# Norm factors multiplied in on ScalarE inside the seven-product loop, a reordered loop entry, and a last projection whose second half comes out token by row

## The chip, the cores and the metric

One core of a Trainium2 chip runs the whole program in one launch. The metric is device time in microseconds (us). Instructions run on TensorE (PE; PEld is its weight load), VectorE (DVE), ScalarE (ACT), GpSimd (POOL) and SyncE (SP, which here only issues transfers). ScalarE and GpSimd issue transfers too.

## The reference, cut to what matters

A token sequence of 1024 with width 1024 passes through two blocks. The first ends in a feed-forward part; the second has a retention layer and a differential attention layer:

```python
up = causal_depthwise_conv(rms_norm(x, norm2_g) @ w_up, ffn_dw_w)      # 2 x 2816 channels
gate, val = jnp.split(up, 2, axis=-1)
x = x + (jax.nn.silu(gate) * val) @ w_down
# layer 0 of the second block: retention
x = x + rmsnorm((retention(...) * silu(gate)) @ w_out_a, post_norm[0])
# layer 1: differential attention
q, gate = split(rmsnorm(x, pre_norm[1]) @ w_in_b)
k, v = split(rmsnorm(x, kv_norm) @ w_kv)
y = (rmsnorm(diff_attention(q, k, v, lam), sub_norm_b) * (1 - lambda_init) * silu(gate)) @ w_out_b
x = x + rmsnorm(y, post_norm[1])                                       # the output
```

All of it is float32. `pre_norm[1]` and `kv_norm` are factors per input row of `w_in_b` and `w_kv`; `post_norm[1]` is a factor per output channel.

## The kernel before, in words

Activations lie with channels on the 128 partitions and tokens along the free axis: `A` has 8 tiles of 128 x 1024. Every float32 product is made of three fast ones (`mm3`): operands are split in a high part (`HH`, `WH`) and the rest (`HL`, `WL`). Weights come in units of 128 x 2048 floats, 1 MB each. In most phases a unit is transferred twice, by the SyncE queue to `RAW` and by GpSimd's queue to `WH`, and DVE then makes `WL` = `RAW` - `WH` (`low_part`, L269). `RAW` has one buffer, `WH` and `WL` have two. A new `RAW` transfer waits until the previous `low_part` is done; a new `WH` transfer waits until TensorE has begun the unit in the other buffer.

The feed-forward part has three stages. Its first four weight tiles are plain products (`ffn_first`). The other 18 tiles, t = 4 to 21, go through the seven-product loop (`up_pe`, `up_act`, `up_dve`): seven products M0 to M6 of 12 matmuls each replace eight, on sums of quarters of the weights ("pieces", built by GpSimd into `WLF`, split by ScalarE into `WH` and by DVE into `WL`, L1993) and on sums of quarters of the activations ("mixes", `XF`, built by GpSimd at L2115, split into `XH` and `XL`, L1981). M4 waits for ScalarE's copy `m2` of bank 0, M5 for DVE's `q`, M6 for DVE's `r` (L2201). The convolution taps of a tile are DVE's L2002; the next tile but one may not begin before they are done. The first tile of the loop is `j` = 0, so the second (`j` = 1) waits for the taps of plain tile 3. The third stage (`ffn_last`, `down_pe`) is the down projection in 22 units of 48 matmuls; ScalarE makes `WH` there (L2281) and DVE `WL` (L2286). The stage also reloads `A` and brings in the 22 tiles that the loop stored (`us_in`).

During this third stage the 16 units of `w_in_b` and `w_kv` get their norm factors: GpSimd's queue loads a unit to `gs` (two buffers), DVE multiplies it in two instructions (`gain_unit`, L2482), and GpSimd's queue stores it to the DRAM tensor `gu` (`gains_pool`), from where the attention phase reads its weights.

The differential attention runs over eight heads; in its last head (`diff_last`) parts of the last projection are slipped in. The last projection (`w_out_b`, `last_pe`) works on 8 output tiles of 128 channels, and does tokens 0 to 511 first, then tokens 512 to 1023. The sum of squares over channels is a product with a matrix of ones; then come a logarithm and an exponential on ScalarE, and for each of 8 tiles DVE's L632 (times factor and root) and L637 (plus `x`), and the stores.

## Time and profile before

| | us |
|---|---|
| median of 3 runs | 2733.58 (2727.04 to 2734.06) |
| the profiled execution | 2728.09 |
| its span, first to last instruction | 2726.4 |
| TensorE busy | 2652.7 |
| DVE busy | 1677.9 |
| ScalarE busy | 875.2 |
| GpSimd busy | 494.9 |

TensorE is busy nearly all the time, so the stages are read for the places where it is not, or where it is at the lower of its two clock levels. Busy time of the other engines matters only at such places.

### The profile page before, as it was taken

How to read it: one execution, taken by the hardware profiler on the slowest of the kernel's cores; microseconds unless marked ns; L12 is line 12 of the kernel's file. 1: busy time of each engine (PE TensorE's matmuls, PEld its weight loads, DVE VectorE, ACT ScalarE, POOL GpSimd, SP SyncE). 2: the span in 40 equal slices, each digit the busy share in tenths (PEclk: the TensorE clock that was granted, in tenths of full speed). 3: DMA queues.
4: the chain of work that ended last, by engine and by line, in shares of the span. 5: the costliest groups of instructions: out<-in, count | busy, mean ns of one | idle time of the engine just before them, and what ended most of it. 6: DMA issues, size and time to landing. Idle time of an engine off the chain costs nothing.

```text
span 2726.4 us, 35637 instructions
## 1 busy us (share of the span) xinstructions
PE 2652.7 (97%) x13108; PEld 2138.8 (78%) x13124; DVE 1677.9 (62%) x2240; ACT 875.2 (32%) x1580; POOL 494.9 (18%) x423
## 2 busy tenths in 40 slices
PE   9999989989999999999999999999999999999987
PEld 7767757877888878788888888888877888888775
DVE  8955563768888865445444345345376666666655
ACT  5333341333444433232112112112144444444441
POOL 0899900153333200121000000000000000000000
PEclk9999999999999999999999999999999999999999
DMA  5211114322222389742222222222244222222124
GB/s 194 77 63 61 52 57 150 113 101 78 85 77 85 150 333 340 264 172 91 77 92 77 77 92 77 77 92 77 78 154 143 78 77 77 77 77 77 58 78 155
DMA packets 59944, 300.42 MB, mean 110 GB/s; under 512 B 7648, under 2 KB 8800, under 8 KB 32224
## 3 DMA queue, kind: packets, MB, share of 16 engines
q1 hardware_dynamic: 34160, 154.53, 16.0%
q0 software_dynamic: 14976, 109.06, 11.8%
q10 hardware_dynamic: 10736, 35.86, 3.4%
q8 instruction: 48, 0.79, 0.1%
q14 instruction: 24, 0.20, 0.0%
HBM read 245.93 MB, written 45.09 MB: 107 GB/s over the span
## 4 chain that ended last, share of the span: by engine, by line
PE 78%; DMA 7%; DVE 6%; issue 2%; ACT 1%; POOL 1%; SPq 0%; DVEq 0%; ACTq 0%; POOLq 0%
PE OBB L253 9%; PE OBB L255 9%; PE OBB L254 9%; DMA gu<-gs 6%; PE PB L253 4%; PE PB L255 4%; PE PB L254 4%; PE TBB L253 4%; PE TBB L255 4%; PE TBB L254 4%; PE TBB L979 3%; PE PB L1028 2%; PE OBB L1093 2%; PE PB L1945 2%; PE PB L1947 2%; PE PB L1946 2%
## 5 line engine op out<-in xcount | busy, mean ns | idle before, releaser
L253 PE MATMUL OBB<-HH,WH 128*128 128x512 f32 x752 | 306.3, 407 | 4.2 <-issue 3.0
L255 PE MATMUL OBB<-HH,WL 128*128 128x512 f32 x752 | 295.6, 393 | 0.0
L254 PE MATMUL OBB<-HL,WH 128*128 128x512 f32 x752 | 295.3, 393 | 0.0
L3143 POOL DMA_DIRECT2D WH<-units x56 | 30.4, 542 | 1184.4 <-PE OBB L253 734.2
L253 PE MATMUL PB<-HH,WH 128*128 128x512 f32 x560 | 227.0, 405 | 1.6 <-DVE hc L903 1.0
L255 PE MATMUL PB<-HH,WL 128*128 128x512 f32 x560 | 218.3, 390 | 0.0
L254 PE MATMUL PB<-HL,WH 128*128 128x512 f32 x560 | 218.1, 389 | 0.0
L269 DVE TENSOR_TENSOR WL<-RAW,WH 128x2048 fp32r<-128x2048 f32 x72 | 170.0, 2361 | 73.1 <-DMA WH<-units 71.3
L1228 ACT ACTIVATE E<-PB,small 128x128 f32<-128x128 f32 (+3 forms) x192 | 141.1, 738 | 224.5 <-DVE small L1324 218.2
L1324 DVE TENSOR_REDUCE small<-PB 128x1 f32<-128x128 f32 (+3 forms) x192 | 138.7, 752 | 61.2 <-PE PB L1046 61.1
L253 PEld LDWEIGHTS OBB<-HH,WH 128*128 128x128 f32 x752 | 142.9, 190 | 32.4 <-issue 4.0
L255 PEld LDWEIGHTS OBB<-HH,WL 128*128 128x128 f32 x752 | 142.4, 189 | 32.0
L2107 POOL TENSOR_TENSOR WLF<-RAW 128x512 f32<-128x512 f32 x90 | 124.6, 1387 | 232.9 <-PE PB L1947 109.8
L254 PEld LDWEIGHTS OBB<-HL,WH 128*128 128x128 f32 x752 | 143.0, 190 | 26.6
L2789 ACT ACTIVATE vr<-OBB,rtok 128x256 f32<-128x256 f32 x32 | 15.3, 477 | 353.1 <-PE OBB L255 353.1
L253 PEld LDWEIGHTS PB<-HH,WH 128*128 128x128 f32 x560 | 105.2, 188 | 28.9 <-issue 5.0
L3176 POOL TENSOR_TENSOR cacc<-cacc,prod 128x498 f32<-128x498 f32 (+29 forms) x94 | 126.4, 1345 | 0.0
L254 PEld LDWEIGHTS PB<-HL,WH 128*128 128x128 f32 x560 | 105.2, 188 | 25.7 <-issue 4.8
L3165 POOL TENSOR_TENSOR prod<-hc,par 128x498 f32<-128x498 f32 (+29 forms) x94 | 123.3, 1312 | 6.8
L255 PEld LDWEIGHTS PB<-HH,WL 128*128 128x128 f32 x560 | 105.1, 188 | 22.3
L1945 PE MATMUL PB<-XH,WH 128*128 128x512 f32 x252 | 101.0, 401 | 11.7 <-ACT m L2155 8.1
L1993 DVE TENSOR_TENSOR WL<-WLF,WH 128x512 fp32r<-128x512 f32 x90 | 105.1, 1170 | 0.0
(456 smaller groups left out, 6277.8 us busy)
## 6 DMA issues: line engine op xcount, KB each, us to landing
RAW<-units SPq DMA_DIRECT2D x78, 1024.0 KB, 4.9
WH<-units POOLq DMA_DIRECT2D x56, 1024.0 KB, 5.1
RAW<-ups SPq DMA_DIRECT2D x18, 1024.0 KB, 4.8
gs<-units POOLq DMA_DIRECT2D x16, 1024.0 KB, 7.7
gu<-gs POOLq DMA_DIRECT2D x16, 1024.0 KB, 10.8
RAW<-gu SPq DMA_DIRECT2D x16, 1024.0 KB, 4.9
WH<-gu POOLq DMA_DIRECT2D x16, 1024.0 KB, 5.1
ub<-V SPq DMA_DIRECT2D x22, 512.0 KB, 2.6
```

Of the source, the lines that this page charges most:

```text
L253: first = pe.e.matmul(out, wh, xh, start=start, stop=False)
L254: pe.e.matmul(out, wh, xl, start=False, stop=False)
L255: return pe.e.matmul(out, wl, xh, start=False, stop=stop), first
L269: dve.e.tensor_tensor(WL[s][:, :], RAW[:, :], WH[s][:, :].bitcast(F32), ALU.subtract).then_inc(unit_split, 1)
L979: mm = pe.e.transpose(dst[:, c * P:(c + 1) * P], src(b), c_("ident"))
L1228: e.activation((E0, E1)[c][:, 0:n], PB[c][:, 0:n], ACT.Exp, bias=small[:, c, t:t + 1], accum_out=small[:, 2 + c, t:t + 1]).then_inc(act_do ...
L1324: e.tensor_reduce(small[:, c, t:t + 1], PB[c][:, 0:(t + 1) * P], AX, ALU.max, negate=True).then_inc(dve_done, dve.mark(f"m{c}_{t}"))
L1945: pe.e.matmul(bank(j, n), wh, XH[p][:, k, :], start=p < 4 and k == 0, stop=False, skip_group_check=True)
L1993: dve.e.tensor_tensor(piece(WL, p), source, piece(WH, p).bitcast(F32), ALU.subtract).then_inc(dve_done, dve.mark(f"w{p}_{j}"))
L2107: pool.tensor_tensor(piece(WLF, p), raw_quarter(t % 2, a), raw_quarter(t % 2, b), op).then_inc(summed, 1)
L3165: ins = pool.tensor_tensor(prod[:, n % 2, 0:b - a], hc[:, c, a - d:b - d], weight.to_broadcast([P, b - a]), ALU.mult)
L3176: pool.tensor_tensor(cacc[:, c, a:b], cacc[:, c, a:b], prod[:, n % 2, 0:b - a], ALU.add).then_inc(conv_taps, 1)
```

## The change

Three parts.

First, the norm factors. `gains_pool` and DVE's `gain_unit` go. For the tiles t = 5 to 20 of the seven-product loop ScalarE's `gain_unit` multiplies one unit in place, as 16 instructions of 128 x 128 with a factor per partition, between piece 2 and piece 3 of the tile. SyncE's queue stores the unit to `gu`, waits until that has landed, and loads the next one to `gs`, which now has one buffer.

Second, the entry of that loop. Mixes 3 and 5 are built by DVE (`mix_sum`) and no longer by GpSimd; the copy `m2` and the combinations `q`, `r`, `ra` of the first loop tile come ahead of the taps of plain tile 3; the Silu and the gate product of plain tile 3 come behind.

Third, the last projection. Tokens 0 to 511 are still made with channels on the partitions, from units `U_WOB` to `U_WOB + 3`, cut so that the first two hold output tiles 0 to 3. Tokens 512 to 1023 are made with tokens on the partitions: the activation tile is the stationary operand and a weight row block of 512 columns the moving one, in four units `U_WOB + 4` to `+ 7`, each used for all four token tiles `j`. So the last matmuls of the four token tiles fall close together. Squares are then summed along the free axis by ScalarE, the root is a number per partition, and DVE needs two L632-like and two L637-like instructions for each token tile. The input `x` for these tokens is loaded at the start of the last head and turned there by TensorE (`x_turn_pe`, 32 transposes), in place of six filler matmuls; ScalarE takes it out of the banks. Eight units are brought in, where five were. The output is assembled from two tensors by the host.

```diff
+            for n in range(4):
+                slot = unit(pe, U_WOB + 4 + n)
+                for j in range(4):
+                    if n == 0 and j == 2:
...
+                        pe.e.wait_ge(dve_done, at_mark(pe, "dve", "acc7"))
+                        pe.e.matmul(OB[0], ones[:, :], last_square(0), start=True, stop=True).then_inc(
+                            pe_done, pe.mark("total"))
+                    if n == 0 and j < 3:
+                        pe.e.wait_ge(dve_done, at_mark(pe, "dve", f"y{2 * j + 1}_0"))
+                    if n == 0 and j == 3:
+                        pe.e.wait_ge(act_done, at_mark(pe, "act", "ln"))
+                    tokens = slice(HALF + j * P, HALF + (j + 1) * P)
+                    for b in range(2):
+                        for r in range(2):
+                            k, c = 2 * n + r, r * 1024 + b * HALF
...
+                for n in range(4):
+                    e.dma_start(xf[:, 2 * n:2 * n + 2, :], xs_pieces()[n][:, :, half_of(0)]).then_inc(x_again[n], 16)
...
+                e.wait_ge(pe_done, at_mark(act, "pe", f"z{j}_{b}"))
+                if j:
+                    e.wait_ge(act_done, at_mark(act, "act", f"zq{j - 1}_{b}"))
+                e.activation(sql[:, b, :], TOKEN_BANKS[j][b], ACT.Square, scale=D ** -0.5,
+                             accum_out=small[:, b, j:j + 1]).then_inc(act_done, act.mark(f"zq{j}_{b}"))
...
+                e.wait_ge(dve_done, at_mark(act, "dve", f"bias{j}"))
+                e.activation(small[:, 3, j:j + 1], small[:, 1, j:j + 1], ACT.Ln, bias=small[:, 2, j:j + 1]).then_inc(
+                    act_done, act.mark(f"zl{j}"))
+                e.wait_ge(act_done, at_mark(act, "act", f"zl{j}"))
+                e.activation(small[:, 4, j:j + 1], small[:, 3, j:j + 1], ACT.Exp, scale=-0.5).then_inc(
+                    act_done, act.mark(f"zr{j}"))
...
+            def token(j, b):
+                e.wait_ge(act_done, at_mark(dve, "act", f"zr{j}"))
+                out = A[:, 2 * j + b, half_of(1)]
+                e.scalar_tensor_tensor(out, TOKEN_BANKS[j][b], small[:, 4, j:j + 1], gainb[:, half_of(b)],
+                                       ALU.mult, ALU.mult).then_inc(dve_done, dve.mark(f"zs{j}_{b}"))
+
+            def token_add(j, b):
+                e.wait_ge(dve_done, at_mark(dve, "dve", f"zs{j}_{b}"))
+                out = A[:, 2 * j + b, half_of(1)].rearrange("p (k n) -> p k n", n=P)
+                e.tensor_tensor(out, out, xt[b][:, :, j * P:(j + 1) * P], ALU.add).then_inc(
+                    dve_done, dve.mark(f"z{j}_{b}"))
+
+            low_part(dve, U_WOB + 2)
...
+            low_part(dve, U_WOB + 5)
+            for k in range(4):
+                tile(k)
+            low_part(dve, U_WOB + 6)
+            for k in range(4, KT):
...
+            low_part(dve, U_WOB + 7)
+            e.wait_ge(tok_in[2], 16)
+            bias(0)
+            for j in range(4):
+                token(j, 0)
+                token(j, 1)
+                if j < 3:
+                    bias(j + 1)
+                token_add(j, 0)
+                token_add(j, 1)

...
-                for n in range(3):
-                    act.e.dma_start(XRB[:, 2 * n:2 * n + 2, :], xs_pieces()[n]).then_inc(x_again[n], 16)
-                act.e.dma_start(XRB[:, 6, :], xs_pieces()[3][:, 0, :]).then_inc(x_again[3], 16)
-                act.e.dma_start(xr7[:, :], xs_pieces()[3][:, 1, :]).then_inc(x_again[3], 16)
             for k in range(KT):
...
             if not more and not forget:
+                unit(pe, U_WOB + 1)
                 for k in (4, 5):
-                    whole_pe(pe, U_WOB, k, k == 4)
+                    pe.e.wait_ge(dve_done, at_mark(pe, "dve", f"lo{k}"))
+                    last_whole(pe, k)
...
+                low_part(dve, U_WOB + 1)
...
+            for m in range(4):
+                c = m * HALF + (k - 4) * P
+                last, first = mm3(pe, FIRST_BANKS[m], WH[slot][:, c:c + P], WL[slot][:, c:c + P],
+                                  HH[:, k, half_of(0)], HL[:, k, half_of(0)], k == 4, k == KT - 1)
...
+        TURN_BANKS = {1: ((0, TB[1]), (1, HIGH_PB[0])), 2: ((2, TB[1]), (3, HIGH_PB[0]), (4, HIGH_PB[1])),
+                      3: ((5, TB[1]), (6, DB[:, :]), (7, HIGH_PB[0]))}
...
+        def x_load(act):
+
+            act.e.wait_ge(spilled, 16 + 64)
+            for n in range(2):
+                act.e.dma_start(xt[n][:, :, :], io["xs"].rearrange("(k p) s -> p k s", p=P)[
+                    :, 4 * n:4 * n + 4, half_of(1)]).then_inc(tok_in[n], 16)
+            act.e.dma_start(gainb[:, :], io["gain"]).then_inc(tok_in[2], 16)
...
+            for k, bank in TURN_BANKS[t]:
+                act.e.wait_ge(pe_done, at_mark(act, "pe", f"xt{k}"))
+                act.e.activation(xt[k // 4][:, k % 4, :], bank, ACT.Copy).then_inc(act_done, act.mark(f"xe{k}"))

...
-            for p in (3, 4, 5):
-                mix_high(act, p)
...
             e.wait_ge(pe_done, at_mark(act, "pe", "v3"))
             for p in (4, 5):
                 piece_high(act, p, 1, UP_FIRST)
+            mix_high(act, 5)
             gate_value(3)
+            e.wait_ge(dve_done, at_mark(act, "dve", "x1"))
+            e.wait_ge(summed, FIRST_SUMS["x6"])
+            e.wait_ge(pe_done, done_in("pe", UP_PHASES[0], "M0_0"))
+            e.activation(m2[:, 0, :], bank(0, 0), ACT.Copy).then_inc(act_done, act.mark("m2_f"))
             mix_high(act, 6)
             e.wait_ge(summed, FIRST_SUMS["p6"])
             piece_high(act, 6, 1, UP_FIRST)
...
             product(2)
+            mix_sum(dve, 3, "h1")
             for p in range(4):
                 piece_low(dve, p, 1, UP_FIRST, None)
+            mix_sum(dve, 5, "h5")
             mix_low(dve, 3)
+            scaled(3)
...
-            mix_low(dve, 5)
-            scaled(3)
             for p in (4, 5):
                 piece_low(dve, p, 1, UP_FIRST, None)
+            mix_low(dve, 5)
...
+                e.tensor_tensor(out, bank(0, product), b, op).then_inc(dve_done, dve.mark(name))
+
+            e.wait_ge(act_done, at_mark(dve, "act", "m2_f"))
+            combined("q_f", 1, None, qb[:, 0, :], m2[:, 0, :], ALU.add)
+            mix_low(dve, 6)
+            combined("r_f", 2, "q_f", rb[:, 0, :], qb[:, 0, :], ALU.subtract)
+            piece_low(dve, 6, 1, UP_FIRST, None)
+            combined("ra_f", 3, "r_f", rb[:, 0, :], rb[:, 0, :], ALU.add)
             taps_of(3)
...
-            for p, name in ((3, "h1"), (4, "h3"), (5, "h5"), (6, "v3")):
+            for p, name in ((4, "h3"), (6, "v3")):
...
+            def gain_unit(j, i):
+
+                e.wait_ge(gain_in, counted(act, i, 32, 16 * j))
+                for n in range(2 * KT):
+                    part = gs[:, n * P:(n + 1) * P]
+                    ins = e.activation(part, part, ACT.Copy, scale=p_(("pre_b", "kvn")[n // KT], n % KT, 1))
+                ins.then_inc(act_done, act.mark(f"gain_{j}"))
...
+                            e.wait_ge(dve_done, done_in("dve", "ffn_first", f"cg_{tag(UP_FIRST - 1)}"))
+                            e.activation(G0[:, :], G0[:, :], ACT.Silu).then_inc(act_done, act.mark("si_f"))
+                        else:
+                            gain_unit(j, i)
...
+                j, r = t % 2, t - UP_FIRST - 1
+                if 0 <= r < 2 * DIFF_HEADS:
+                    sp.wait_ge(act_done, up_at("act", t, f"gain_{j}"))
+                    sp.dma_start(io["gu"][r], gs[:, :]).then_inc(gain_out, 16)
                 if t < FF_TILES - 1:
-                    sp.wait_ge(summed, 10 + 5 * (t + 1 - UP_FIRST))
+                    sp.wait_ge(summed, FIRST_SUMS["p6"] + 5 * (t + 1 - UP_FIRST))
...
+                if r + 1 < 2 * DIFF_HEADS:
+                    if t == UP_FIRST:
+                        sp.wait_ge(u_out[(t - 1) % 2], 16 * (t // 2))
+                    else:
+                        sp.wait_ge(gain_out, 16 * (r + 1))
+                    sp.dma_start(gs[:, :], io["units"][U_DIFF + r + 1]).then_inc(gain_in, 16)
...
-                pool.dma_start(gs[r % 2][:, :], io["units"][U_DIFF + r]).then_inc(gain_in[r % 2], 16)
-
-            pool.wait_ge(pe_done, up_at("pe", FF_TILES - 1, "M0_1"))
-            load(0)
-            load(1)
-            for r in range(2 * DIFF_HEADS):
-                pool.wait_ge(dve_done, done_in("dve", "ffn_last", f"gain{r}1"))
-                pool.dma_start(io["gu"][r], gs[r % 2][:, :]).then_inc(gain_out[r % 2], 16)
-                if r + 2 < 2 * DIFF_HEADS:
-                    pool.wait_ge(gain_out[r % 2], 16 * (r // 2 + 1))
-                    load(r + 2)
-
-        def gain_unit(dve, r):
-            dve.e.wait_ge(gain_in[r % 2], 16 * (r // 2 + 1))
-            for j in range(2):
-                part = gs[r % 2][:, j * 1024:(j + 1) * 1024].rearrange("p (k n) -> p k n", k=KT)
-                dve.e.tensor_tensor(part, part, p_(("pre_b", "kvn")[j]).unsqueeze(2).to_broadcast([P, KT, P]),
-                                    ALU.mult).then_inc(dve_done, dve.mark(f"gain{r}{j}"))
```

On DVE, at the entry of the loop, this stood before, from the piece differences of the first loop tile on (XL: rest of a mix; WL: rest of a piece; rbx and par: scaling and taps of plain tile 3):

```order
L1993 TENSOR_TENSOR WL_58<-WLF_128,WH_56 128x512 x4
L1981 TENSOR_TENSOR XL_143<-XF_147,XH_139 128x2048
L1981 TENSOR_TENSOR XL_144<-XF_148,XH_140 128x2048
L1981 TENSOR_TENSOR XL_145<-XF_149,XH_141 128x2048
L2063 TENSOR_TENSOR TBB<-TBB,rbx 128x1024
L2063 TENSOR_TENSOR OBB<-OBB,rbx 128x1024
L1993 TENSOR_TENSOR WL_59<-RAW,WH_57 128x512 x2
L2002 SCALAR_TENSOR_TENSOR G_151<-TBB,par,G_151 128x1023
L2002 SCALAR_TENSOR_TENSOR G_151<-TBB,par,G_151 128x1022
L2002 SCALAR_TENSOR_TENSOR V_152<-OBB,par,V_152 128x1023
L2002 SCALAR_TENSOR_TENSOR V_152<-OBB,par,V_152 128x1022
L1981 TENSOR_TENSOR XL_146<-XF_150,XH_142 128x2048
```

And this stands there now (L2055: `mix_sum`; L2190: `combined` of the first loop tile):

```order
L2055 TENSOR_TENSOR XF_151<-A 128x2048
L2072 TENSOR_TENSOR WL_57<-WLF_131,WH_55 128x512 x4
L2055 TENSOR_TENSOR XF_153<-A 128x2048
L2060 TENSOR_TENSOR XL_147<-XF_151,XH_143 128x2048
L2146 TENSOR_TENSOR TBB<-TBB,rbx 128x1024
L2146 TENSOR_TENSOR OBB<-OBB,rbx 128x1024
L2060 TENSOR_TENSOR XL_148<-XF_152,XH_144 128x2048
L2072 TENSOR_TENSOR WL_58<-RAW,WH_56 128x512 x2
L2060 TENSOR_TENSOR XL_149<-XF_153,XH_145 128x2048
L2190 TENSOR_TENSOR qb<-PB,m_159 128x512
L2060 TENSOR_TENSOR XL_150<-XF_154,XH_146 128x2048
L2190 TENSOR_TENSOR rb<-PB,qb 128x512
```

Two mixes have come in, and `qb` and `rb`, for which M5 and M6 wait, stand ahead of the taps, which begin three instructions after the last row shown.

On ScalarE, this stood before in the second tile of the loop (m: the copy for which M4 waits; WH: pieces 0 to 3 of the next tile, then 4 and 5):

```order
L2155 ACTIVATE m_155<-OBB 128x512
L1987 ACTIVATE WH_56<-WLF_128 128x512 x4
L1987 ACTIVATE WH_57<-RAW 128x512 x2
L2166 ACTIVATE carry<-epsc 128x1
L2167 ACTIVATE V<-OBB,par 128x1024
L2171 ACTIVATE carry<-epsc 128x1
L2172 ACTIVATE G<-TBB,par 128x1024
```

And now:

```order
L2258 ACTIVATE m_159<-OBB 128x512
L2066 ACTIVATE WH_55<-WLF_131 128x512 x3
L2240 ACTIVATE gs<-gs,par 128x128 x16
L2066 ACTIVATE WH_55<-WLF_131 128x512
L2066 ACTIVATE WH_56<-RAW 128x512 x2
L2276 ACTIVATE carry<-epsc 128x1
L2277 ACTIVATE V<-OBB,par 128x1024
L2281 ACTIVATE carry<-epsc 128x1
```

The 16 instructions on `gs` stand between piece 2 and piece 3, and what follows them on ScalarE waits for them.

At the end of the program DVE had this before, for the last five of eight output tiles of the second half of the tokens (L632 times factor and root, L637 plus `x`), all of it behind the last matmul and the root:

```order
L632 SCALAR_TENSOR_TENSOR tmn<-OBB,par,rbn 128x512
L637 TENSOR_TENSOR A<-tmn,XRB 128x512
L632 SCALAR_TENSOR_TENSOR tmn<-PB,par,rbn 128x512
L637 TENSOR_TENSOR A<-tmn,XRB 128x512
L632 SCALAR_TENSOR_TENSOR tmn<-PB,par,rbn 128x512
L637 TENSOR_TENSOR A<-tmn,XRB 128x512
L632 SCALAR_TENSOR_TENSOR tmn<-TBB,par,rbn 128x512
L637 TENSOR_TENSOR A<-tmn,XRB 128x512
L632 SCALAR_TENSOR_TENSOR tmn<-TBB,par,rbn 128x512
L637 TENSOR_TENSOR A<-tmn,xr_55 128x512
```

And now, for the last two token tiles (L648: `token`, L654: `token_add`, L642: `bias`):

```order
L648 SCALAR_TENSOR_TENSOR A<-TBB,small,gainb 128x512 x2
L642 TENSOR_TENSOR small<-small,epsc 128x1
L654 TENSOR_TENSOR A<-A,xt_78 128x512
L654 TENSOR_TENSOR A<-A,xt_79 128x512
L648 SCALAR_TENSOR_TENSOR A<-OBB,small,gainb 128x512 x2
L654 TENSOR_TENSOR A<-A,xt_78 128x512
L654 TENSOR_TENSOR A<-A,xt_79 128x512
```

Eight tiles' worth of instructions behind the last matmul have become one token tile's: the last three rows, four instructions.

## Rows read from the trace of the kernel before

**Rows 1.** The page's head and its first part.

```profile
span 2726.4 us, 35637 instructions
...
PE 2652.7 (97%) x13108; PEld 2138.8 (78%) x13124; DVE 1677.9 (62%) x2240; ACT 875.2 (32%) x1580; POOL 494.9 (18%) x423
```

**Rows 2.** Busy time by stretch: length, engines, granted clock, DMA share, GB/s.

```profile
602.40:627.40 25.00, 13.28 (x38) 10.18 (x38) 22.05 (x23) 10.81 (x14) 10.98 (x7) 0.73 0.27 106
627.40:952.80 325.40, 325.40 (x1426) 267.48 (x1425) 277.14 (x304) 137.19 (x218) 111.44 (x83) 1.00 0.26 96
952.80:1165.00 212.20, 203.66 (x881) 165.58 (x880) 120.18 (x112) 65.33 (x70) 24.92 (x33) 0.99 0.83 306
2563.80:2639.00 75.20, 66.94 (x370) 51.32 (x371) 43.96 (x72) 34.78 (x77) 0.53 (x1) 0.95 0.04 15
2639.00:2706.50 67.50, 66.31 (x291) 54.23 (x290) 31.96 (x40) 10.39 (x17) 1.58 (x3) 1.00 0.52 187
2706.50:2726.40 19.90, 1.86 (x5) 0.38 (x3) 10.92 (x16) 1.91 (x3) 0.00 (x0) 0.68 0.29 106
```

**Rows 3.** Timeline at the loop's entry: start, us, instruction, idle before and releaser.

```profile
578.83 6.86 DVE L1993 TENSOR_TENSOR WL<-WLF,WH 128x512 fp32r<-128x512 f32 x4
...
599.19 2.68 DVE L1981 TENSOR_TENSOR XL<-XF,XH 128x2048 fp32r<-128x2048 f32 x1 [4.39 <-ACT XH L1975]
...
606.38 2.59 DVE L2002 SCALAR_TENSOR_TENSOR G<-TBB,par,G 128x1023 f32<-128x1023 f32 x2
...
610.60 0.80 PE L1945 MATMUL PB<-XH,WH 128*128 128x512 f32 x1 [8.07 <-ACT m L2155]
...
619.00 0.80 PE L1945 MATMUL PB<-XH,WH 128*128 128x512 f32 x1 [3.66 <-DVE qb L2201]
```

**Rows 4.** Timeline of the second loop tile, ScalarE's piece 3 and DVE.

```profile
640.01 0.63 ACT L1987 ACTIVATE WH<-WLF 128x512 fp32r<-128x512 f32 x1 [2.27 <-POOL WLF L2107]
...
641.66 0.68 DVE L2201 TENSOR_TENSOR qb<-OBB,qb 128x512 f32<-128x512 f32 x1
...
646.57 0.70 DVE L2201 TENSOR_TENSOR TBB<-TBB,qb 128x512 f32<-128x512 f32 x1 [1.36 <-PE TBB L1947]
```

**Rows 5.** Timeline of ScalarE: a 128 x 128 instruction and its successor.

```profile
2627.40 0.31 ACT L3012 ACTIVATE sqd<-ot 128x128 f32<-128x128 f32 x1
2627.61 0.19 ACT L3012 ACTIVATION_READ_ACCUMULATOR sqd<-ot 128x1 f32 x1
```

**Rows 6.** Waits in the down projection (952 to 1165 us).

```profile
DVE gs L2482 <- DMA gs<-units: 72.7, 14, 8.6
...
PE PB L253 <- DVE WL L2286: 4.9, 4, 1.7
```

**Rows 7.** Transfers of 900 to 1165 us: KB each, median us to landing.

```profile
gs<-units POOLq DMA_DIRECT2D x16, 1024.0 KB, 7.7
gu<-gs POOLq DMA_DIRECT2D x16, 1024.0 KB, 10.8
```

**Rows 8.** Transfers of 640 to 900 us, the same columns.

```profile
RAW<-ups SPq DMA_DIRECT2D x14, 1024.0 KB, 4.8
ub<-V SPq DMA_DIRECT2D x13, 512.0 KB, 2.6
```

**Rows 9.** Timeline of the last projection and of the end.

```profile
2639.72 0.53 POOL L3143 DMA_DIRECT2D WH<-units  x1 [42.85 <-PE TBB L253]
...
2648.59 2.29 DVE L269 TENSOR_TENSOR WL<-RAW,WH 128x2048 fp32r<-128x2048 f32 x1 [3.56 <-DMA WH<-units]
...
2650.93 0.50 PE L253 MATMUL OBB<-HH,WH 128*128 128x512 f32 x1 [1.19 <-DVE WL L269]
...
2652.06 0.53 POOL L3143 DMA_DIRECT2D WH<-units  x1 [11.81 <-PE OBB L253]
...
2659.05 2.29 DVE L269 TENSOR_TENSOR WL<-RAW,WH 128x2048 fp32r<-128x2048 f32 x1 [1.63 <-DMA WH<-units]
...
2720.56 0.69 DVE L637 TENSOR_TENSOR A<-tmn,xr 128x512 f32<-128x512 f32 x1
```

381 lines of the change are left out of this document (194 added, 187 removed).

## The prediction

> **What bounds the kernel now.** I read the head of the page first: TensorE is busy 2652.7 of 2726.4 us [rows 1]. So a gain can only come from places where it waits, where its clock is low, or from the end, where it has finished. The busy time by stretch shows the three that the change touches [rows 2]. At the loop's entry, 602.4 to 627.4 us, it is busy 13.3 of 25.0 us at a mean granted clock of 0.73. In the down projection, 952.8 to 1165, it is busy 203.7 of 212.2 us while the DMA engines are 0.83 busy. After 2706.5 it has next to nothing to do for 19.9 us. In between, the loop has no gap at all: 325.4 of 325.4 us at clock 1.00, with DMA at 0.26. The reader is to see that the same transfers and multiplications that crowd one stage would have room in the other.
>
> **The norm factors leave the down projection.** Removed are 32 DVE instructions, 16 loads and 16 stores of 1 MB. DVE waited 72.7 us for loads to `gs`, up to 8.6 at a time, and what is queued behind such a wait is `WL` of the next unit, for which TensorE then waited 4.9 us [rows 6]. The other waits there come from `RAW` and `us_in` landing late on full queues: a 1 MB load took 7.7 us and a store 10.8 [rows 7], against 4.8 for a load in the loop [rows 8]. All in all TensorE loses 212.2 - 203.7 = 8.5 us by gaps and 0.01 x 212 = 2 us by the clock [rows 2], together 10.6. The upper end of the gain is 10.6. The lower end is 4: a first gap (the fill of the stage) and the one while `A` and the stored tiles come back may stay, since those transfers stay. I take 9, since without 32 MB the stage needs about half of what it moves now.
>
> **They enter the loop.** Per tile ScalarE gets 16 instructions of 128 x 128. Such an instruction lasts 0.31 us and the next starts 0.21 us after it [rows 5]; 16 x 0.21 + 0.1 = 3.5 us. Behind them are queued pieces 3, 4 and 5, for which DVE waits, and behind those on DVE the combinations that free the banks. In the row, piece 3 starts at 640.01, 2.27 us after ScalarE was last busy (637.74) [rows 4]. With the factors between, it starts at 637.74 + 3.5 = 641.2, so 1.2 us late. DVE's instruction after piece 3, at 641.66, becomes about 1.2 us late, and DVE then waits 1.36 us for TensorE at 646.57 [rows 4]. The delay ends there, and TensorE sees nothing: cost 0 per tile, hidden by DVE's wait. Without that cover it would be 1.2 x 16 = 19 us. ScalarE itself has room: 137 of 325 us busy, plus 16 x 3.5 = 56 [rows 2]. The first loop tile that does this may start it late; I put 0.5 us.
>
> The Trainium skill, "ScalarE: Activation LUTs", section Rules for kernel authors, says that multiplications belong on VectorE and that an instruction on ScalarE is to be budgeted at some 0.3 us plus 0.83 ns per element. An estimate by it is 16 x 0.41 = 6.5 us per tile; piece 3 would then be 4.2 us late, DVE about 2 us late behind the cover, and the loop would stand near the edge. The start-to-start time of the row decides against that figure, and I keep 3.5.
>
> Transfers in the loop grow by 2 MB per tile of 325.4/17 = 19.1 us. The store comes first, then the load waits until the store has landed, then ScalarE multiplies: a ring. With 4.8 us for a load, about the same for a store (0.5 MB took 2.6) [rows 8], and 3.5 for ScalarE it is 13 us, under 19.1. The load also stands behind `RAW` of a later tile on SyncE's queue and behind GpSimd's last piece, so it may land near the moment when ScalarE wants it; up to 1 us late would still be covered.
>
> **The entry.** TensorE waits 8.07 us for `m` and 3.66 us for `qb` [rows 3]. M4 to M6 take 3 x 12 x 0.228 = 8.2 us at the loop's pace (325.4 us for 17 x 84 matmuls [rows 2]), but took 25 from 602.4; 16.8 us are lost, 11.7 in gaps and 5 by the clock. Now `m` stands ahead of the Silu and waits only for M0 and GpSimd's mix 6. GpSimd has two mixes fewer, so `m` is ready before 602.4 and the first gap goes. Then DVE is late next. From 578.8 it has, in its new order: a mix (2.5), four pieces (6.9 [rows 3]), a mix (2.5), four rests of mixes (2.7 each [rows 3], the first one longer), scaling 2.4 (2048 columns, at 0.68 us for 512 [rows 4] less three starts), two pieces 2.4, `q`, `r`, `ra` (0.7 each [rows 4]) and piece 6 (1.7, as one of the four at 578.8), and the taps, 2 x 2.6 [rows 3]; together 37 us, to 616. A mix of 128 x 2048 is not in the trace on DVE; the nearest row is the rest of a mix, same size, same number of operands, 2.7 us. `q` comes at about 605 and costs nothing, `r` and piece 6 at about 610, some 2 us late. M0 of the next tile waits for the taps and its piece 0: 616.5, against 627.2 before. The gap before it is about 4 us, like the one at 619.00; the two gaps of before cost 5 us by the clock, so this one 2.2 to 2.5; I put 2.2. The gain is 627.2 - 616.5 - 2.2 = 8.5; I take 9 since the low clock may be shorter. Bounds: 12 if DVE is never slowed by GpSimd's additions and the clock stays up, 5 if each DVE step there is a fifth slower.
>
> **The last projection.** The matmuls are as many as before, and six units of 48 still come behind the last head. What changes is the end. Before, from 2706.5, a product with ones, a logarithm, an exponential and 16 DVE instructions up to 2721.25 [rows 9], then 5.15 us until the last store has landed and the program ends at 2726.4 [rows 1]. Now the last token tile needs, after the last matmul, a square of 512 columns (0.6, as the 0.63 in [rows 4], and 0.2 to read its sum [rows 5]), a logarithm and an exponential of one column (0.2 each at least, as that read; with waits 0.7), and DVE's four instructions. DVE takes 2.9 us per token tile (four of 0.7 [rows 9], and a small one), and TensorE delivers one each 12 x 0.228 = 2.7 us, so DVE lags a little: it ends about 4.9 us after the last matmul. With 5.15 us for the store this makes 10.0 instead of 19.9: gain 9.9 (8 to 11).
>
> What it costs: units follow each other every 48 x 0.228 = 10.9 us, and 2 MB must come in for each. A `WH` transfer issued beside its `RAW` landed 8.9 us after issue in one place (2639.72 to 2648.59), and TensorE stood 1.19 us; it landed after 7.0 us in the other (2652.06 to 2659.05), and TensorE did not stand [rows 9]. With 1.1 us before the issue and 2.3 for `WL`, the unit is there 12.3 or 10.4 us after the one before began. Before, only two hand-overs had this form; now there are five or six, one of them beside 2 MB of `x`. Bounds: -1 (no gap at all) and +9 (six gaps of 1.4 instead of one, and 2 for `x`). I take +1.5, nearer the faster row, as nothing else was on the queues there either. Two exchanges in the last head, `low_part` of the second unit ahead of the last transposes and 32 transposes for six fillers, lie where TensorE stands 8.3 of 75.2 us anyway [rows 2]; at most as long as 32 wide matmuls, 7 us, at least minus 2. I put +0.5.
>
> The Trainium skill, "DMA: Bandwidth & Descriptors", section Anatomy of one DMA, gives 2.0 us plus bytes over 436 GB/s. An estimate by it for the pair is 2.0 + 4.8 = 6.8 us, so a unit every 10.2 us and no gap; the last stage would cost 0 and the sum be 1.5 lower. The row of 7.0 agrees with it, the row of 8.9 does not.
>
> **The sum**, against the profiled execution's own 2728.1: - 9 (down projection) + 0.5 (loop) - 9 (entry) - 9.9 (end) + 1.5 + 0.5 (last projection, last head) = 2701.7. The median of the runs stands 5.5 us above that execution, and the runs spread from 2727.0 to 2734.1, so I forecast 2703.
>
> **The rivals.** (a) The ring becomes the bound. If loads and stores in the loop take what they took in the down projection, the ring is 7.7 + 10.8 + 3.5 + 0.7 for two issues = 22.7 us, 3.6 above a tile. Over 15 rounds that is +54: 2757, slower. It decides from a ring of 19.1 us on, so from 15 us for store and load. Against it stands the DMA share of 0.26 in the loop. (b) The last projection becomes bound by its transfers at the slower row: +9 instead of +1.5, 2710 to 2712. For it speaks that each late unit makes both transfers of the next start together again. (c) The entry hardly gains, because GpSimd and DVE disturb each other and the low clock returns: 2707 to 2709. (d) The gaps of the down projection stay, being made by `A` and `us_in`: 2708. (e) ScalarE's factors are not covered, 1.2 us per tile: 2722, still faster. (f) The change does nothing: only if (e) and (b) come together.
>
> **How the numbers follow.** Forecast, all three gains within their bounds: 0.62, 2695 to 2709. One of (b), (c), (d) or two of them in part: 0.24, up to 2717. (e): 0.06. (a): 0.05. No change: 0.03. The range 2694 to 2716 holds somewhat over 8 in 10. A measurement of this kernel tells 0.3%, 8 us, from no change: faster 0.92, same 0.03, slower 0.05.
>
> **What would show it.** In the profile after: the PE wait for `m` gone, and one gap of 3 to 5 us before the second loop tile; loop tiles 19.1 us apart, and no SyncE or ScalarE wait for `gs` that reaches TensorE; fewer than 3 us of gaps in the down projection; the last matmul about 10 us before the end; gaps before units of the last projection of 0 to 1.5 us. Tiles 20 us or more apart would show (a) or (e), and regular gaps of over 1 us behind 2640 would show (b).

## The result, and the profile after

| | before | after |
|---|---|---|
| median of the runs, us | 2733.82 (4 runs) | 2693.96 (4 runs, 2691.51 to 2696.82) |
| ratio, 95% interval | | 0.9864 (0.9852 to 0.9876) |
| the same once more, later | 2731.70 (9 runs) | 2699.76 (5 runs), 0.9874 (0.9856 to 0.9891) |
| the profiled execution, us | 2728.09 | 2696.82 |
| its span | 2726.4 | 2695.2 |

One of the four runs of the kernel before took 11960.6 us; it is left out of the ratio. The change makes the kernel 1.26 to 1.36 per cent faster, by 34 to 37 us. The forecast was 2703 with a range from 2694 to 2716: right in sign, with a time 3 to 9 us too long. The first median, 2693.96, lies on the lower edge of the range, the second inside it. The two medians of this one kernel are 5.8 us apart, so a difference of less than some 6 us between two medians below says little.

The head of the page, beside [rows 1]:

```profile
span 2695.2 us, 35949 instructions
...
PE 2647.1 (98%) x13124; PEld 2139.3 (79%) x13140; DVE 1642.8 (61%) x2211; ACT 951.5 (35%) x1858; POOL 466.3 (17%) x386
```

Busy time by stretch of the changed kernel, for the same six places as [rows 2] (length, engines, granted clock, DMA share, GB/s):

```profile
602.40:614.80 12.40, 8.67 (x38) 6.55 (x37) 12.33 (x12) 4.71 (x8) 9.75 (x5) 0.97 0.22 81
614.80:943.40 328.60, 328.58 (x1426) 269.82 (x1427) 280.48 (x312) 209.53 (x476) 109.09 (x80) 0.99 0.50 193
943.40:1146.00 202.60, 200.58 (x881) 164.83 (x880) 84.28 (x80) 65.59 (x70) 7.21 (x3) 1.00 0.46 167
2546.15:2621.10 74.95, 66.17 (x387) 53.28 (x388) 45.34 (x72) 38.55 (x85) 1.06 (x2) 0.93 0.22 78
2621.10:2688.50 67.40, 67.15 (x293) 54.47 (x291) 38.99 (x50) 12.48 (x30) 2.65 (x5) 1.00 0.65 227
2688.50:2695.20 6.70, 0.00 (x0) 0.00 (x0) 3.90 (x8) 1.19 (x5) 0.00 (x0) 0.82 0.62 233
```

The reader is to see three stretches that shrank: the entry from 25.0 to 12.4 us, the down projection from 212.2 to 202.6, the end from 19.9 to 6.7. The loop's DMA share rose from 0.26 to 0.50 and the down projection's fell from 0.83 to 0.46: the 32 MB have moved to where there was room. The loop is 3.2 us longer, and the factors are not the reason: from the first matmul of its fourth tile to its last matmul it takes 287.57 us in both profiles (tiles 19.19 us apart). The 3.2 us are the second tile, 22.14 us instead of 19.19 behind the gap at 614.82 (granted clock 0.50 from 614.8 to 620.5), and 0.2 by where the stretches were cut.

One profile against one profile hides what chance does. So I cut every profiled run at the same five matmuls, by their rows: the first of the seven-product loop, the first of the down projection (`UH`; the wait before it falls in the loop's column), the product with ones of the retention phase (`sqr`, after its first norm), the first scores of the last head, and the last matmul of the projection. The differences of their times, in us:

| run | to the loop | loop | down projection and on | attention | last head and projection | end | span |
|---|---|---|---|---|---|---|---|
| before | 591.35 | 363.90 | 1064.18 | 544.37 | 142.75 | 19.85 | 2726.4 |
| after | 591.46 | 354.41 | 1054.59 | 545.69 | 142.32 | 6.73 | 2695.2 |
| after_again | 596.24 | 352.90 | 1054.59 | 542.42 | 142.44 | 6.71 | 2695.3 |
| undo_gains | 596.69 | 355.17 | 1069.24 | 545.43 | 143.63 | 6.84 | 2717.0 |
| undo_entry | 597.84 | 362.18 | 1054.53 | 543.95 | 140.43 | 6.67 | 2705.6 |
| undo_last | 591.24 | 353.42 | 1054.56 | 544.39 | 142.30 | 17.29 | 2703.2 |
| work_only | 591.50 | 354.05 | 1054.37 | 544.28 | 141.98 | 6.72 | 2692.9 |
| moves_only | 592.38 | 357.45 | 1066.69 | 545.37 | 140.60 | 6.71 | 2709.2 |
| order_only | 594.38 | 358.31 | 1054.41 | 544.27 | 141.81 | 6.72 | 2699.9 |
| entry2 | 591.61 | 356.64 | 1054.40 | 543.75 | 143.45 | 6.65 | 2696.5 |
| mixes_dve | 597.52 | 352.16 | 1054.66 | 545.66 | 142.76 | 6.64 | 2699.4 |
| mixes_dve2 | 595.51 | 354.72 | 1054.54 | 544.06 | 140.53 | 6.64 | 2696.0 |
| gains_x15 | 592.38 | 367.89 | 1055.58 | 545.15 | 142.93 | 6.67 | 2710.6 |
| gains_x2 | 596.10 | 387.00 | 1056.41 | 543.98 | 139.03 | 6.98 | 2729.5 |

Read by column, it says what is chance. No run changed the part to the loop, and it lies between 591.2 and 597.8. The third column is 1054.4 to 1054.7 in all eight runs that have nothing extra in the loop or in that stage; there a difference of 1 us is real. The loop's column has 1 to 2 us of chance (352.9 and 354.4 for the same kernel), and that of the last head and projection more: 139.0 to 143.6 in the runs that have the new last projection.

The entry, in the timeline of the changed kernel (beside [rows 3]):

```profile
599.68 0.60 ACT L2126 ACTIVATE m<-PB 128x512 f32<-128x512 f32 x1 [3.06 <-issue]
...
600.07 3.39 DVE L2060 TENSOR_TENSOR XL<-XF,XH 128x2048 fp32r<-128x2048 f32 x1
603.38 0.68 DVE L2190 TENSOR_TENSOR qb<-PB,m 128x512 f32<-128x512 f32 x1
...
606.68 0.68 DVE L2190 TENSOR_TENSOR rb<-PB,qb 128x512 f32<-128x512 f32 x1
...
608.56 0.47 PE L2012 MATMUL PB<-XH,WH 128*128 128x512 f32 x1 [0.48 <-DVE WL L2072]
...
614.82 0.77 PE L2012 MATMUL OBB<-XH,WH 128*128 128x512 f32 x1 [3.28 <-DVE WL L2072]
```

`m` is ready 10 us earlier than before, TensorE waits 0.48 us for piece 6 and 3.28 us before the second loop tile, and for nothing else there.

A loop tile of the changed kernel, ScalarE and DVE (beside [rows 4, 5]):

```profile
704.98 4.78 ACT L2240 ACTIVATE gs<-gs,par 128x128 f32<-128x128 f32 x16
709.67 0.61 ACT L2066 ACTIVATE WH<-WLF 128x512 fp32r<-128x512 f32 x1
...
710.32 0.69 DVE L2072 TENSOR_TENSOR WL<-WLF,WH 128x512 fp32r<-128x512 f32 x1 [1.85 <-ACT WH L2066]
...
714.00 0.70 DVE L2314 TENSOR_TENSOR TBB<-TBB,qb 128x512 f32<-128x512 f32 x1 [0.58 <-PE TBB L2014]
```

The 16 factors take 709.67 - 704.98 = 4.69 us, and piece 3 starts 2.3 us later in the tile than before (15.16 us behind its first matmul, 12.84 before). DVE's wait for TensorE, 1.36 us before [rows 4], is down to 0.58, but it is still there. Before, DVE waited twice for TensorE behind piece 3; the first wait, which is now gone, is this one:

```profile
643.85 0.70 DVE L2201 TENSOR_TENSOR OBB<-TBB,rb 128x512 f32<-128x512 f32 x1 [0.92 <-PE TBB L1947]
```

The transfers of the loop after (614 to 942 us, beside [rows 7, 8]):

```profile
gs<-units SPq DMA_DIRECT2D x16, 1024.0 KB, 7.0
gu<-gs SPq DMA_DIRECT2D x16, 1024.0 KB, 3.9
RAW<-ups SPq DMA_DIRECT2D x15, 1024.0 KB, 4.9
```

And all that TensorE still waits for in the down projection (942.7 to 1146 us, beside [rows 6]):

```profile
PE PB L253 <- DVE WL L2405: 1.8, 1, 1.8
...
PE PB L253 <- DVE UL L2390: 0.3, 1, 0.3
```

### The profile page after: what moved, and what is told of

It reads as the page before. It is cut to its first block, busy times and chain, and to the rows that moved or that the text cites. A ratio compares the mean times of both kernels' runs of the same rounds, so it can differ in the third digit from the quotient of the medians.

```text
span 2695.2 us, 35949 instructions
## 1 busy us (share of the span) xinstructions
PE 2647.1 (98%) x13124; PEld 2139.3 (79%) x13140; DVE 1642.8 (61%) x2211; ACT 951.5 (35%) x1858; POOL 466.3 (17%) x386
## 4 chain that ended last, share of the span: by engine, by line
PE 86%; DVE 6%; issue 2%; ACT 1%; DMA 1%; SPq 0%; DVEq 0%; ACTq 0%; POOLq 0%
PE OBB L253 10%; PE OBB L255 9%; PE OBB L254 9%; PE PB L253 5%; PE PB L255 5%; PE PB L254 5%; PE TBB L253 4%; PE TBB L255 4%; PE TBB L254 4%; PE TBB L994 3%; PE PB L1043 2%; PE OBB L1110 2%; PE PB L2012 2%; PE PB L2014 2%; PE PB L2013 2%
## 5 line engine op out<-in xcount | busy, mean ns | idle before, releaser
L253 PE MATMUL OBB<-HH,WH 128*128 128x512 f32 x736 | 300.2, 408 | 3.2 <-issue 3.0
L255 PE MATMUL OBB<-HH,WL 128*128 128x512 f32 x736 | 289.4, 393 | 0.0
L254 PE MATMUL OBB<-HL,WH 128*128 128x512 f32 x736 | 289.2, 393 | 0.0
L269 DVE TENSOR_TENSOR WL<-RAW,WH 128x2048 fp32r<-128x2048 f32 x75 | 178.1, 2375 | 83.8 <-DMA WH<-units 82.2
L253 PE MATMUL PB<-HH,WH 128*128 128x512 f32 x528 | 214.2, 406 | 2.8 <-DVE HL L415 1.8
L255 PE MATMUL PB<-HH,WL 128*128 128x512 f32 x528 | 205.8, 390 | 0.0
L254 PE MATMUL PB<-HL,WH 128*128 128x512 f32 x528 | 205.6, 389 | 0.0
L2405 DVE TENSOR_TENSOR WL<-RAW,WH 128x2048 fp32r<-128x2048 f32 x22 | 51.9, 2358 | 130.2 <-ACT WH L2400 130.1
L253 PEld LDWEIGHTS PB<-HH,WH 128*128 128x128 f32 x528 | 99.1, 188 | 28.4 <-issue 4.7
L254 PEld LDWEIGHTS PB<-HL,WH 128*128 128x128 f32 x528 | 99.2, 188 | 24.5 <-issue 4.5
L255 PEld LDWEIGHTS PB<-HH,WL 128*128 128x128 f32 x528 | 99.1, 188 | 21.2
```

The costliest lines, as they stand in the source:

```text
L253: first = pe.e.matmul(out, wh, xh, start=start, stop=False)
L254: pe.e.matmul(out, wh, xl, start=False, stop=False)
L255: return pe.e.matmul(out, wl, xh, start=False, stop=stop), first
L269: dve.e.tensor_tensor(WL[s][:, :], RAW[:, :], WH[s][:, :].bitcast(F32), ALU.subtract).then_inc(unit_split, 1)
```

## The experiments

All are edits of the changed kernel unless said otherwise; ratios are to the kernel before, measured beside it.

**undo_gains.** Part one of the change put back, parts two and three kept.

```diff
-                        else:
-                            gain_unit(j, i)
...
+                if u < 2 * DIFF_HEADS:
+                    gain_unit(dve, u)
...
+            gains_pool(pool)
```

> The changed kernel with only the norm factors put back where they were (DVE multiplies them in the down projection, GpSimd's queue moves the 32 MB); entry and last projection stay changed. The changed kernel's down projection has one gap of 1.76 us and clock 1.00, and between its start and the next phase it gained 9.6 us on the kernel before. My theory, that transfers and multiplications on full queues made the gaps: four or five gaps come back, DVE waits some 70 us for gs, and the kernel is 9 to 10 us slower than the changed one (2703 to 2706, profile 2705). Rival, that the gaps came from A and us_in as before and vanished only because the phase is entered with other leads: less than 3 us. ScalarE's share of the loop falls by some 75 us without any effect on TensorE.

Measured: 0.9915 (0.9902 to 0.9929), that is 11 to 14 us slower than the changed kernel. In the table it is the third column, 1069.24 against 1054.59. TensorE has eight gaps from its first matmul on, of 0.4 to 3.3 us, and DVE waits 77.5 us for `gs`. That the factors made the gaps holds; the size is somewhat larger than I had said, and larger than before the change (1064.18). Its five runs spread over 14 us (2704.28 to 2718.72), those of the changed kernel over 5 and 8, and its profile is of the slowest of the five.

**work_only** and **moves_only.** Which half of it makes the gaps, DVE's work or the transfers? Each is added alone to the changed kernel's down projection: in work_only two products of 128 x 1024 in place (the first two lines), in moves_only the loads and stores (the others).

```diff
+                if u < 2 * DIFF_HEADS:
+                    gain_work(dve, u)
...
+                    pool.dma_start(io["gx"][r - 2], gz[r % 2][:, :]).then_inc(extra_out[r % 2], 16)
...
+                    pool.dma_start(gz[r % 2][:, :], io["units"][U_DIFF + r]).then_inc(extra_in[r % 2], 16)
```

> The changed kernel with 32 extra DVE multiplications (128 x 1024 in place, two per unit of the down projection, where the factors stood before) and no extra transfer. Nothing is left out. By my theory, that the transfers made the gaps of the down projection, DVE's 16 x 2.4 = 38 us of work lie in its waits for ScalarE's WH (113 us in the changed kernel): at most 1 us slower than the changed kernel (2694 to 2695 as its own median; below 0.04%). Rival, that DVE's place in the chain WH, WL makes the gaps: 2.4 us more between WH and a second unit's WL, gaps of 1 us and more per unit, 5 to 14 us slower.

> The changed kernel with 16 extra loads and 16 extra stores of 1 MB by GpSimd's queue in the down projection (each store behind its load, two buffers, to a DRAM tensor that nobody reads), with no DVE work and no wait of any engine but GpSimd for them, before unit 17. Nothing is left out. By my theory gaps come back as with the whole part put back: 9 to 14 us slower than the changed kernel (2703 to 2708), with RAW and us_in landing late. Rival, DVE's waits for gs (72.7 us before) and its multiplications made the gaps: under 3 us.

Measured: work_only 0.9872 (0.9857 to 0.9887), third column 1054.37: nothing. moves_only 0.9932 (0.9918 to 0.9945), 16 to 19 us slower, more than the 9 to 14 I had put; its third column is 1066.69, 12 us more, and its first gap of 5.59 us adds 3 to 4.5 to the loop's column. Its issues, one of its waits and two of TensorE's rows:

```profile
RAW<-units SPq DMA_DIRECT2D x18, 1024.0 KB, 9.9
...
us_in<-ub SPq DMA_DIRECT2D x44, 256.0 KB, 8.7
```

```profile
ACT WH L2403 <- DMA RAW<-units: 34.1, 4, 13.2
```

```profile
949.83 0.79 PE L255 MATMUL PB<-UH,WH 128*128 128x512 f32 x1 [5.59 <-DVE WL L2408]
...
1004.06 0.77 PE L255 MATMUL PB<-UH,WH 128*128 128x512 f32 x1 [6.06 <-DVE UL L2393]
```

A load of `RAW` lands after 9.9 us, where in the changed kernel it takes 4.9. Both gaps end on DVE, which stands behind ScalarE; before the gap at 1004.06 ScalarE waited 13.2 us for such a load, before that at 949.83 it waited 9.8 us for `us_in`. So crowded transfers alone can make a loss, and DVE's work alone makes none. This path was in the kernel before too: ScalarE waited 15.18 us for `RAW` there, and TensorE's gap behind it was 2.73 us (at 1002.58).

The early loss of moves_only can't be taken over in size, since its extra stores begin at 935.20, those of the kernel before at 971.01. And moves_only has three gaps, the last at 1004, and none of the later ones. In its second part the extra transfers still run, the DMA engines are 0.85 busy (0.80 in the kernel before, 1030 to 1165 us), and TensorE has no gap:

```profile
1020.00:1130.00 110.00, 110.00 (x485) 90.70 (x485) 41.77 (x41) 31.16 (x32) 8.98 (x17) 1.00 0.85 303
```

In the kernel before TensorE stood there at 1093.43, 1116.89 and 1139.27 for 1.56, 1.34 and 0.32 us, and each time DVE had just come out of a wait for `gs`:

```profile
1112.28 2.36 DVE L2482 TENSOR_TENSOR gs<-gs,par 128x1024 f32<-128x1024 f32 x2 [8.60 <-DMA gs<-units]
1114.55 2.28 DVE L2286 TENSOR_TENSOR WL<-RAW,WH 128x2048 fp32r<-128x2048 f32 x1
1116.89 0.50 PE L253 MATMUL PB<-UH,WH 128*128 128x512 f32 x1 [1.34 <-DVE WL L2286]
```

ScalarE had `WH` ready long before (it waited for TensorE), so what was late was DVE's factor product behind the load, and `WL` behind that. Undo_gains has five such gaps, 5.1 us together, behind waits for `gs` of 5.2 to 9.6 us. So DVE's waits for `gs` [rows 6], which I had read as the first link, were the last link of 3.2 of the 4.9 us that TensorE waited for `WL`; 1.73 of them are the first gap, which stayed. This path needs the late load and DVE's work behind it, and neither half has it alone; no run adds only DVE's wait.

**gains_x2** and **gains_x15.** How much cover have the factors? Behind the 16 factors come 16 copies in place, 8 in gains_x15.

```diff
+                e.wait_ge(act_done, at_mark(act, "act", f"factor_{j}", i))
+                for n in range(16):
+                    part = gs[:, n * P:(n + 1) * P]
+                    ins = e.activation(part, part, ACT.Copy)
```

> The changed kernel with 16 more ScalarE instructions of 128 x 128 per loop tile (copies in place, factor 1), behind the 16 of the factors: nothing is left out. They take 4.7 us more per tile. By my theory the factors are covered only by DVE's wait for TensorE behind piece 3, of which 0.58 us is left: (4.7 - 0.6) x 16 = 66 us slower, tiles 23.3 us apart. Rival, the ring of store, load and ScalarE is what binds: 9.5 + 3.9 + 7.0 + 0.2 = 20.6 us per tile, 1.4 over 19.2, 21 us slower. Second rival, TensorE's buffers hide more than DVE's wait shows: less than 40.

> The changed kernel with 8 extra copies of 128 x 128 in place behind the factors of each loop tile. 16 such copies made piece 3 3.34 us later and the tile 1.97 us longer, so 1.37 us of lateness were hidden. If that is a fixed slack, 8 copies (1.7 us) cost 0.3 us per tile, 5 us in all; tiles 19.5 us apart. If instead a share of each added us reaches TensorE (59 per cent in that run), they cost 1.0 us per tile, 16 us in all.

Measured: gains_x2 0.9999 (0.9989 to 1.0008), 34 to 37 us slower than the changed kernel where my theory said 66; gains_x15 0.9917 (0.9901 to 0.9932), 12 to 14 us slower. ScalarE's rows of one tile of gains_x2, and TensorE's wait in it:

```profile
823.97 4.79 ACT L2240 ACTIVATE gs<-gs,par 128x128 f32<-128x128 f32 x16
828.78 3.31 ACT L2245 ACTIVATE gs<-gs 128x128 f32<-128x128 f32 x16
832.00 0.62 ACT L2066 ACTIVATE WH<-WLF 128x512 fp32r<-128x512 f32 x1
```

```profile
822.63 0.49 PE L2012 MATMUL PB<-XH,WH 128*128 128x512 f32 x1 [1.68 <-ACT m L2263]
```

Piece 3 comes 832.00 - 823.97 - 4.69 = 3.34 us later, and the tile takes 21.16 us instead of 19.19, 1.97 more. With 8 copies it is 1.75 us later and the tile 19.95, 0.76 more. So 1.0 to 1.4 us more than the factors would have stayed hidden, and none of my lines is right (all but 0.6; a fixed 1.37, so 0.3 per tile; 59 per cent, so 1.0 per tile). TensorE's wait for `m` suggests why DVE's 0.58 was not the whole cover: lateness passes from piece 3 to DVE's combinations, to the taps, to the Silu, and to the `m` behind it on ScalarE, and it reaches TensorE at M4. In gains_x15 most of the short waits end on DVE's `qb` instead. Both runs also pay at the first matmul of the down projection, which waits 4.4 and 4.8 us instead of 1.8. The ring did not bind: no wait for `gs` in either run.

**undo_entry** and **order_only.** Part two put back whole; and the new order kept with mixes 3 and 5 by GpSimd.

```diff
-            for p, name in ((4, "h3"), (6, "v3")):
+            for p, name in ((3, "h1"), (4, "h3"), (5, "h5"), (6, "v3")):
...
-            mix_sum(dve, 3, "h1")
-            mix_sum(dve, 5, "h5")
```

> The changed kernel with only the entry of the seven-product loop put back (GpSimd builds mixes 3 and 5, m, q, r behind the taps of plain tile 3). By my theory the gaps of 8 and 3.7 us and the low clock come back, so it is 11 us slower than the changed kernel (12.4 in the arrival of the second loop tile's M0, less what the low clock behind the one gap of now costs, 2.6): 2704 to 2707. Rival, that the factors on ScalarE or the other moves made the entry quick: under 5 us.

> The changed kernel with mixes 3 and 5 built by GpSimd again, but the new order kept (m, q, r ahead of the taps of tile 3). Before, GpSimd ended mix 6 at 604.2 and M4's operands m was 610.0 behind the gate product's copies and a Silu. By my theory (GpSimd's two mixes fewer are what brings mix 6, and with it m, ahead of TensorE) a gap of 4 to 5 us before M4 stays, with the low clock: 5 to 7 us slower than the changed kernel. Rival, the order alone does it: under 2 us slower.

Measured: undo_entry 0.9895 (0.9880 to 0.9910), 6 to 9 us slower, less than my 11 (12.4 less 2.6 is 9.8, so 11 was also a slip); loop column 362.18 against 352.9 to 354.4, 8 to 9 us. The two gaps came back (8.09 us for `m`, 3.23 for `qb`). order_only 0.9884 (0.9869 to 0.9899), column 358.31: 4 to 5 us, about half of it, and a little less than I had put. In order_only TensorE waits 3.33 us for `m` at 608.90, then 2.16 us before M0 of the second tile and 2.45 before its M4. The mixes and the order each carry a part.

**entry2, mixes_dve, mixes_dve2.** The gap of 3.28 us and the low clock behind it seemed worth another 4 to 5 us. Entry2 makes the value taps, then piece 0, then the gate taps (the first three lines); mixes_dve builds mixes 4 and 6 on DVE too (the last two); mixes_dve2 does both.

```diff
-            taps_of(3)
+            tap_marks(dve, 3, 1, V0, None, tag(3))
...
+                        low(0)
...
+            mix_sum(dve, 4, "h3")
...
+            mix_sum(dve, 6, "v3")
```

> A version meant to be faster. In the changed kernel the second loop tile's M0 waits 3.27 us for DVE's piece 0, which stands behind all four taps of plain tile 3, and the 1.2 GHz that follows costs 2.6 us. M0 writes a value bank, M1 is the first to write a gate bank. So DVE now does the value taps, piece 0 of that tile, then the gate taps and the other pieces; TensorE waits for the gate taps only before M1. By my theory M0 comes at 612.2 instead of 614.8, the gap is 0.6 us and the clock stays at 2.4 GHz: 4 to 5 us faster than the changed kernel. Rival, M1 now waits as long for the gate taps (ready 2.5 us later): a gain under 1 us.

> A version meant to be faster: mixes 4 and 6 are built by DVE too, so GpSimd builds no mix between tile 3's first product and the loop. In the changed kernel DVE is busy without a break from 578.7 to 632 us, and beside GpSimd's mixes its instructions are long: four piece differences 6.89 us (0.68 each alone), a rest of a mix 3.39 (2.28 alone). By my theory, that the entry is as long as DVE's work in it, DVE gets 2 x 2.28 us more and loses 4.2 + 2.2 + 1.1 us of slowing: 3 us less. M0 of the second loop tile then comes 3 us earlier, at TensorE's own pace, with no gap of over 0.5 us and no low clock there: 3 to 5.5 us faster than the changed kernel. Rival, GpSimd's next pieces move into the same time and slow DVE as the mixes did: under 1 us gained, or up to 2 us lost.

> The version just named together with the order of taps of the run entry2 (value taps, piece 0, gate taps). If DVE's backlog is what bounds the entry, the order of the taps only moves the wait, and this equals the version just named within 1 us. If its M0 still waits for the taps there, this one is up to 2.6 us faster.

> The changed kernel once more, beside the three that follow. Median 2693 to 2696, ratio to the kernel before 0.986.

Measured: entry2 0.9876 (0.9860 to 0.9891), mixes_dve 0.9871 (0.9852 to 0.9890), mixes_dve2 0.9868 (0.9851 to 0.9884), after_again 0.9874 (0.9856 to 0.9891), its median 2699.76 where I had put 2693 to 2696. None is faster than the changed kernel, where I had put 4 to 5 us for entry2 and 3 to 5.5 for mixes_dve. TensorE in entry2:

```profile
612.47 0.47 PE L2012 MATMUL OBB<-XH,WH 128*128 128x512 f32 x1 [0.77 <-DVE WL L2076]
...
629.28 0.80 PE L2012 MATMUL OBB<-XH,WH 128*128 128x512 f32 x1 [5.18 <-ACT m L2262]
```

M0 came 2.35 us earlier, as computed, and M4 of the same tile then waited 5.18 us for an `m` that stands behind DVE's and ScalarE's backlog. The wait had moved and grown, and the low clock came behind it (granted clock 0.50 from 629.28 to 634). The loop's column is 356.64, 2 to 4 us worse. In mixes_dve2 the same happened: M4 waited 5.23 us. In mixes_dve GpSimd's next piece (597.77 to 600.14) runs beside DVE's mix 6:

```profile
598.89 3.40 DVE L2055 TENSOR_TENSOR XF<-A 128x2048 f32<-128x2048 f32 x1
...
619.41 0.47 PE L2012 MATMUL OBB<-XH,WH 128*128 128x512 f32 x1 [2.54 <-DVE WL L2072]
...
633.09 0.50 PE L2012 MATMUL OBB<-XH,WH 128*128 128x512 f32 x1 [2.42 <-ACT m L2260]
```

M0 of the second tile came 1.5 us earlier behind the loop's first matmul (21.89 us, 23.37 in the changed kernel), not 3. Its loop column, 352.16, is at most 2 us better than the changed kernel's 352.9 to 354.4, which no ratio here can tell.

**undo_last.** Part three put back whole.

> The changed kernel with only the last projection (and its parts in the last head) put back. Last matmul to end: 6.7 us in the changed kernel, 19.9 before; I had forecast 10.0, from 4.9 us of DVE and 5.15 us for the last store as before. If the store's tail belongs to the old form of output, it is 5 us again here and the kernel is 13 to 14 us slower than the changed one (2706 to 2709). If the tail is chance from run to run, it is 2.7 here, and the kernel is 11 us slower. The one gap of 1.2 us before a unit comes back, too.

Measured: 0.9906 (0.9891 to 0.9921), 9 to 11.5 us slower; end column 17.29. DVE's last instruction ends at 2700.61, and the program ends 2.6 us later. With the same code the profile before needed 5.15: its slowest store landed after 4.3 us, those of 256 KB here after 2.0. In all 13 profiles other than that of before, the time from DVE's last instruction to the end is 2.59 to 2.95 us. So 2.5 us of the end of before was chance, and part three is worth 17.29 - 6.73 = 10.6 us at the end, and nothing before it (142.30 and 142.32).

## Why the prediction was right, and where its terms were off

- **Down projection, -9.** Measured -9.6 between profiles, and 11 to 14 by undoing it. That it was the factors' traffic, and that DVE's work alone does nothing, is shown by undo_gains and work_only. The two links that I had named are both in the rows: `RAW` late (2.73 us of gap before) and `WL` queued behind DVE's wait for `gs` (3.2 us); moves_only has only the first. How much each is worth with its share of low clock is open. The first gap stayed (1.76 us), as I had allowed; the one while `A` returns did not.
- **Loop, +0.5.** Measured 0.0: 287.57 us from the fourth tile on in both profiles; the low clock at its start belongs to the entry. The result was right by two errors that cancel. I took 0.21 us per factor from a square followed by an accumulator read [rows 5], and the factors come every 0.29 us: 4.7 us per tile instead of 3.5, so piece 3 was 2.3 us late and not 1.2. By my argument, a cover of 1.36 us, that leaves 2.3 - 1.36 = 0.9 us per tile, an estimate of 15 us in all. It cost nothing, since DVE had a second wait that I had not counted (0.92 us at 643.85, 1.01 in later tiles), 2.3 to 2.4 together, and the whole cycle had 1.0 to 1.4 us more: gains_x15 and gains_x2 show where it ends. By the Trainium skill's sum of 6.5 us, which I had set against mine, the factors would have been 1.8 us longer still (and piece 3 then 4.2 - 1.36 = 2.8 us late behind my cover, not the 2 that I had put); gains_x15, with 1.75 us more, says what that costs: 0.8 us per tile, 11 us in the loop and 3 to 4 behind it. The Trainium skill, "ScalarE: Activation LUTs", section What ACT_TABLE_LOAD costs, has a finer figure: 186 ns plus 0.833 ns per element, about 93 ns more for each per-partition operand, and back-to-back instructions overlapping by about 93 ns. An estimate by it is 0.29 us with the factor and 0.20 without; the trace agrees with both (4.69 / 16 = 0.29, 3.31 / 16 = 0.21).
- **The ring, 13 us.** 4.7 + 3.9 + 7.0 = 15.6, and `gs` is loaded behind `RAW`'s turn on SyncE's queue (issued at 715.66, landed at 722.6). ScalarE wanted it at 724.17, 1.5 us later. Rival (a) was wrong by its transfer times, which belonged to the crowded stage.
- **Entry, -9.** The column says -9.5 to -11.0 (in it the wait before the down projection, 0.7 us longer in one profile of the changed kernel than in the other), undoing it 6 to 9 us. M0 of the second tile came at 614.82 where I had 616.5, `q` at 603.4 (605), `r` at 606.7 (610), the gap was 3.28 (4), the clock cost 2.95 in this profile and 2.2 in after_again (I had 2.2): here twelve matmuls came 0.43 us apart instead of 0.23. DVE's list of 37 us took 35.4, from 578.67 to 614.07. That DVE is the next to be late is borne out by entry2 and mixes_dve.
- **End, -9.9.** 10.6 by undo_last, 13.1 between the two profiles. What I had taken over as fixed, 5.15 us from DVE's end to the program's, was half chance (2.7 now); DVE itself ends 4.0 us after the last matmul, where I had 4.9.
- **Last projection and last head, +2.0.** -0.4 between the profiles, 0.0 against undo_last, where the column by itself moves by more than that (139.0 to 143.6). The hand-overs were not slower: in the last projection `WH` landed after 6.3 to 7.8 us (median 6.8), so the row of 7.0 was the rule and that of 8.9 the odd one. The 6.8 us estimated from the Trainium skill, "DMA: Bandwidth & Descriptors", section Anatomy of one DMA, fit this median. The one gap between units is this:

```profile
2632.81 0.50 PE L253 MATMUL OBB<-HH,WH 128*128 128x512 f32 x1 [0.22 <-DVE WL L269]
```

The sum itself has a slip: -9 + 0.5 - 9 - 9.9 + 1.5 + 0.5 is -25.4, so it should have read 2702.7 and not 2701.7. Between profiles the difference is -31.2, 5.8 more: 3.2 at the end (2.5 of it chance), 2.4 in the last head and projection, 1.0 in entry and loop, 0.6 in the down projection, less 1.3 that attention took longer and 0.1 before the loop, both chance. The three places and what made them go are as forecast; the prices of the factor and of the store's tail were off, the cover in the loop was argued from one wait of two, and the hand-overs were priced too near the slower row. That 2703 came as near as it did is luck in part. The median of before lay 5.5 us above its profiled execution, and of these I had added only 1.3 to the sum; with the slip put right and the whole 5.5 it would have read 2708. After the change the profiled execution was the slowest of its four runs, 2.9 us above the median. What stays open is why the stage with the factors put back (1069.2) is 5 us longer than in the kernel before (1064.2); one profile of each, that of undo_gains of its slowest run, and a spread of 14 us between runs can't tell it.
